# Dense chunk ahead of scores in every step of an attention stream, and maxima behind the dense part on VectorE

## The reference, cut to what matters

```
s = jnp.einsum('...qkgd,...skd->...kgqs', qg.astype(F32), kk.astype(F32)) * (ATTN_HEAD_DIM ** -0.5) + bias
s = jnp.where(valid, s, -jnp.inf)
sink = sinks.astype(F32).reshape(ATTN_KV_HEADS, ATTN_GROUP, 1)
m = jnp.maximum(jnp.max(s, axis=-1), sink)
e = jnp.exp(s - m[..., None])
p = e / (jnp.sum(e, axis=-1) + jnp.exp(sink - m))[..., None]
return jnp.einsum('...kgqs,...skd->...qkgd', p, vv.astype(F32))
...
x = x + o.astype(x.dtype) @ w_attn_out[j]
```

## Time and profile before

| | |
|---|---|
| median of three runs | 2412.86 us |
| lowest, highest run | 2411.56 us, 2414.92 us |
| the profiled execution | 2408.64 us |
| its span | 2406.8 us |
| TensorE busy | 2324.3 us (97%) |
| VectorE busy | 1489.9 us (62%) |
| ScalarE busy | 978.6 us (41%) |
| mean granted TensorE clock | 0.988 |

### The profile page before, as it was taken

One profiled execution on the slowest core, in us unless ns is written; L12 is line 12 of the kernel. 1 busy time (PEld: TensorE's weight loads), 2 busy tenths in 40 slices (PEclk: granted clock), 3 DMA queues, 4 the chain that ended last, 5 costly groups with the idle time before them and its releaser, 6 DMA issues.

```text
span 2406.8 us, 41163 instructions
## 1 busy us (share of the span) xinstructions
PE 2324.3 (97%) x16202; PEld 2219.4 (92%) x16202; DVE 1489.9 (62%) x2591; ACT 978.6 (41%) x1964; POOL 336.0 (14%) x334
## 2 busy tenths in 40 slices
PE   6999999998999999999998999999999999999998
PEld 6889898878999999999998977878999999999998
DVE  5545555569756656566566676465765656656564
ACT  4232222234535334343343354254633434435345
POOL 4000000013011111112112011013021111111113
PEclk7999999999999999999999999999999999999999
DMA  3112111101111121111111411101112112111121
GB/s 109 53 37 68 49 58 40 42 31 46 36 53 54 35 61 44 50 55 35 56 52 50 104 27 45 38 19 36 44 36 61 45 44 61 35 52 52 35 70 73
DMA packets 160983, 119.71 MB, mean 50 GB/s; under 512 B 23623, under 2 KB 140276, under 8 KB 160836
## 3 DMA queue, kind: packets, MB, share of 16 engines
q1 hardware_dynamic: 160724, 118.10, 16.7%
q10 hardware_dynamic: 144, 0.02, 0.0%
HBM read 110.94 MB, written 12.33 MB: 51 GB/s over the span
## 4 chain that ended last, share of the span: by engine, by line
PE 70%; issue 20%; DVE 5%; POOL 2%; ACT 1%; SPq 0%; POOLq 0%; DMA 0%; DVEq 0%; ACTq 0%
PE acc L2462 9%; PE acc L2464 9%; PE acc L2463 9%; PE acc L2422 8%; PE acc L2423 8%; PE acc L2424 8%; PE acc L2501 3%; PE acc L2503 3%; PE acc L2502 3%; PE acc L2520 2%; PE acc L2543 1%; PE acc L2400 1%; PE acc L2402 1%; PE acc L2401 1%; PE acc L2531 1%
## 5 line engine op out<-in xcount | busy, mean ns | idle before, releaser
L2462 PE MATMUL acc<-h_hi,w_hi 128*128 128x352 f32 x1440 | 464.6, 323 | 6.9 <-DVE x_res L1448 6.9
L2464 PE MATMUL acc<-h_hi,w_lo 128*128 128x352 f32 x1440 | 464.9, 323 | 0.0
L2463 PE MATMUL acc<-h_lo,w_hi 128*128 128x352 f32 x1440 | 462.8, 321 | 0.0
L1448 DVE TENSOR_TENSOR x_res<-x_res,acc 128x1056 f32<-128x1056 f32 x240 | 300.6, 1252 | 127.4 <-PE acc L2464 127.2
L2462 PEld LDWEIGHTS acc<-h_hi,w_hi 128*128 128x128 f32 x1440 | 270.2, 188 | 8.5 <-issue 6.6
L2464 PEld LDWEIGHTS acc<-h_hi,w_lo 128*128 128x128 f32 x1440 | 273.0, 190 | 0.0
L2463 PEld LDWEIGHTS acc<-h_lo,w_hi 128*128 128x128 f32 x1440 | 270.5, 188 | 0.0
L2422 PE MATMUL acc<-x_hi,w_hi 128*128 128x264 f32 x896 | 254.8, 284 | 0.0
L2424 PE MATMUL acc<-x_hi,w_lo 128*128 128x264 f32 x896 | 254.6, 284 | 0.0
L2423 PE MATMUL acc<-x_lo,w_hi 128*128 128x264 f32 x896 | 254.5, 284 | 0.0
L2179 PE MATMUL acc<-x_hi,w_hi 128*128 128x352 f32 x576 | 195.9, 340 | 4.2 <-DVE pair L1651 2.7
(11 more groups left out here) (334 smaller groups left out, 5237.5 us busy)
## 6 DMA issues: line engine op xcount, KB each, us to landing
w_raw<-in_w_up SPq DMA_DIRECT2D x64, 512.0 KB
w_raw<-in_w_down SPq DMA_DIRECT2D x64, 512.0 KB
w_raw<-in_w_mlstm_in SPq DMA_DIRECT2D x24, 512.0 KB
x_in<-in_x_prompt SPq DMA_DIRECT2D x8, 512.0 KB, 3.8
w_raw<-in_w_mlstm_out SPq DMA_DIRECT2D x8, 512.0 KB
w_raw<-in_w_q SPq DMA_DIRECT2D x16, 256.0 KB
w_raw<-in_w_attn_out SPq DMA_DIRECT2D x16, 256.0 KB
out_y_prompt<-y_out SPq DMA_DIRECT2D x8, 512.0 KB, 3.2
```

The costliest lines, as they stand in the source:

```text
L1448: V.tensor_tensor(blocks(x_res[:, k]), blocks(x_res[:, k]), row_banks(layer, k), ALU.add).then_inc(row_taken, 1)
L2462: T.matmul(out[:, b], hi[:, c], mh[:, span(b)], start=(c == 0), stop=False)
L2463: T.matmul(out[:, b], hi[:, c], ml[:, span(b)], start=False, stop=False)
L2464: x = T.matmul(out[:, b], lo[:, c], mh[:, span(b)], start=False, stop=(c == 1))
```

## The change

The two calls are exchanged on TensorE and on VectorE. On TensorE the dense chunks of a step come first, then the scores of unit u+1, the transposes, the values and the sample part. On VectorE the maxima of unit u+1 come behind the dense part instead of ahead of it. No instruction is added or removed, and ScalarE, GpSimd and the DMA queue keep their order.

```
@@ -2087,9 +2087,9 @@  (VectorE)
                     probabilities(u - 1)
                 if u >= 3:
                     outputs(u - 3)
+                att_dense(att_window(u))
                 if u + 1 < UNITS:
                     maxima(u + 1)
-                att_dense(att_window(u))
                 for gp in range(2):
                     sample(gp, u - SAMPLE_AT[gp])
```

## The result

| | before | after |
|---|---|---|
| median | 2413.89 us (6 runs) | 2421.88 us (6 runs) |
| lowest, highest | 2411.56, 2417.88 | 2420.04, 2425.84 |
| ratio | | 1.0034, 95% interval 1.0023 to 1.0045 |
| span of the profiled execution | 2406.8 us | 2418.1 us |

The change makes the kernel 8.0 us slower by the medians, 5.5 to 10.9 by the interval. The forecast was 10.6 us, 2423.5 as a time, added to the median of the three runs known then; with six runs the median before is 1.0 us higher.

A forecast was written before the change was run, and what follows sets the result against it. TensorE, busy 97% of the span, was taken as the bound, with gaps at array-shape changes. Terms 7.8 + 1.7 + 0.8 + 0.2 + 0.6 + 0.3 - 0.8 = 10.6 us, added to 2412.86, gave 2423.5 us; 80% range 2417.5 to 2428.5.

The forecast's parts named there:

- The extra change of shape: TensorE's steps with all four blocks: four array-shape changes instead of three, 0.17 us more in each of 46 steps, +7.8 us.
- The Trainium skill's price: Load of scores behind a dense chunk: by the skill's isolated-matmul latency 0.17 us later, not 0.11, making the shape term 2.8 us larger.
- Sample parts: Steps 24 to 29: TensorE's sample part waits for VectorE's, now behind the maxima; 3.2 us of waits against 1.5, +1.7 us.
- The chunk of step 32: This chunk waits for the low part of the first span's output, without scores ahead: 1.4 us against 0.6, +0.8 us.
- Step 36: Passage from full step 35 to an empty step: scores wait 1.4 us, transposes 0.3, 1.7 in place of 1.1, +0.6 us.
- Step 54: Passage from full step 53 to a step without chunk: scores and transposes wait 0.2 us each, 0.4 against 0.2, +0.2 us.
- Residual: Steps 39 and 42, VectorE's weight split ahead of the add TensorE awaits: +0.3 us in step 39, nothing in step 42.
- Start: Stream's start: step 0's chunk covers the scores' 0.88 us wait for maxima; first load to first transposes 5.0 against 5.82, -0.8 us.
- rival (C): TensorE's clock halves more often: two or three more falls of 3.4 us, each costing 1.7, 2427 to 2428.6 us; 14%.
- (A): TensorE's weight loads are pulled ahead, so the extra shape change costs nothing: +2.8 us, 2415.7 us; 6%.
- (B): VectorE's dense work becomes timely, removing every wait of steps with chunks: 5.2 us gain, 2407.7 us with shape change free; 4%.
- (D): Every added shape change on TensorE costs the widest gap: +15.2 us in place of 7.8, 2430.9 us; 4%.

## Why the prediction was right

*The extra change of shape* was the largest term, 7.8 us. The mechanism is shown, by a run that adds only it (6.5 us) and by a matmul of 64 rows against one of 128. Its size was a little over: 0.17 us a step, 0.15 measured (3.18 us in 21 steps), so 46 x 0.15 = 6.9 us. Chunk to scores, 1.65 us in the stream's first step, is 1.63 in the plain step, and the two starts behind it came 0.01 closer each. Of the bounds, 0.11 and 0.33, the measured value lies near the lower.

*The Trainium skill's price.* In the changed kernel the loads of the scores show the gap of 0.22 us behind the chunk again in every step, that of the earlier trace rows, and the term came out under the rows' sum, not over it. The 2.8 us more that the prediction worked out from the Trainium skill's TensorE: Matmul & The Clock Gate, Single matmul latency, are not there.

*Sample parts.* Forecast 3.2 us of waits in steps 24 to 29 in place of 1.5. Measured 0.53, 0.84, 0.55, 0.56 and 0.79, 3.3 us in all, and 0.27 in step 30, which had been hidden before behind half clock. Right, term by term.

*The chunk of step 32.* Forecast +0.8, measured 1.25 against 0.61, +0.6.

*Step 36.* Forecast a wait of 1.7 in place of 1.1, through GpSimd's old read of `q_t`. Measured:

```profile
1501.37 1.39 DVE L1963 SCALAR_TENSOR_TENSOR q_t<-acc,rstd 128x352 f32<-128x352 f32 x3 [2.67 <-POOL o_lo L1334]
...
1504.14 0.70 PE L2520 MATMUL acc<-k_t,q_t 64*128 64x256 f32 x4 [1.60 <-DVE stat L1997]
```

The moves wait for GpSimd, the scores wait 1.60 us for the maxima behind them, and the transposes' load another 0.1 (a gap of 0.43, where the plain one is 0.33). +0.5.

*Step 54.* Forecast +0.2, from two waits of 0.2 in place of one. Measured +0.1. The view of TensorE's waits shows neither wait, for the modelled ends of the matmuls ahead hide them. The loads show both, 0.2 and 0.1 us beyond the plain gaps of 0.17 and 0.33:

```profile
1609.43 0.30 PEld L2520 LDWEIGHTS acc<-k_t,q_t 64*128 64x128 f32 x4 [0.38 <-DVE stat L1997]
...
1610.16 0.42 PEld L2531 LDWEIGHTS acc<-ident,prob 128*128 128x128 f32 x4 [0.43 <-DVE prob L2007]
```

*Residual.* This step failed: +0.3 was forecast, and the two waits are 0.30 and 0.53 us, where they were 0.33 and 0.57. I had strung the durations of probabilities and outputs together, 0.88 and 0.28 us. In step 39 of the changed kernel their starts lie closer than their ends: the reciprocal starts at 1525.73, the outputs at 1526.46 and the split at 1526.66, 0.93 us and not 1.16. Start-to-start times should have been taken, as for TensorE.

*Start.* Forecast -0.8, measured -0.86.

*Sum.* Measured terms: -0.9 + 6.9 + 1.8 + 0.3 + 0.6 + 0.5 + 0.1 = 9.3 us, inside the interval of 5.5 to 10.9. All terms but the sample parts' came out under their forecast, so the sum isn't right by errors that cancel. The 0.3 in it is the wait of step 30, which the prediction didn't have.

*The clock* makes up the rest of the profiled difference of 11.3 us. Before, it fell in step 30; after, not there but behind the wait of 1.4 us in step 64:

```profile
1637.00:1640.00 3.00, 2.98 (x12) 0.55 0.00 0
```

That is -1.7 and +1.5 us, and one more fall behind the stream, at 1706 us, some 1.7. The 11.3 us are more than the 8.0 of the medians since the profiled execution before lies 5.2 us under its median and the one after 1.8. In rival (C) more waits were to bring more falls; in the changed kernel there were two where there had been one, and the half-clock stretches of the runs above vary as much. One execution of each can't say whether the change does that.

*The signs named ahead.* The four gaps, the sample parts' waits in both spans, the waits of steps 36 and 54 and the start came as forecast; the plain step is 3.44 us and not 3.47, the chunk of step 32 waits 1.25 and not 1.4. One sign of a wrong forecast came too: the time outside the stream moved, by 2.0 us. The fall at 1706 us accounts for most of it, and it is the clock's, which the sum left out.

*Rivals.* (A), loads pulled ahead across a change of shape, is out: at every change of the plain step the load starts together with its first matmul, 2 to 3 ns apart by the medians, where from the chunk to the transposes, without a change, it starts 0.16 us ahead of it. (B), a gain by timely dense work, named waits that did shrink (start, step 36's transposes), but they came back at the scores and the sample parts. (D), the widest gap for each change, is out by the measured 0.15.

## What to carry to other kernels

Read TensorE's list as a sequence of array shapes, not only of dependencies: here 64-row, 64-column and full matmuls in turn paid some 0.15 us for each change added, in gaps that no wait and no busy time shows, so put neighbours of one shape together and count the changes in a loop's cycle. A block whose result is wanted a step later may go anywhere by its dependencies, and still cost by where it stands. A short wait can hide behind the modelled end of a matmul, so ask for the waits of the weight loads too. Before an order on one engine is changed, look also for what it will run beside on GpSimd: here a scaling that started just behind a long GpSimd instruction lasted as long as that one.

## What the hardware showed that was not expected

- VectorE's `TENSOR_SCALAR` on 128x256 float32 took 0.35 us by its median and up to 2.42 us beside GpSimd's subtraction of 2.36; one wait more on GpSimd took 6.7 us off TensorE's waits. In the kernel before the same blocking is there, in five scalings of 1.3 to 1.42 us, but nobody waits; in the changed kernel no scaling takes over 0.66.
- All eleven falls to half clock inside the stream, in the twelve traces, came right behind a wait of 1.0 to 2.4 us among small matmuls; nine were 3.4 us long, one 10.2 and one 13.7. Not each such wait has one: the 1.60 us of step 36 in the changed kernel had none behind it, and 1.62 us at the same place in the run with the sample part ahead of the maxima had. In the kernel before, steps 55 to 63 had eight waits of 0.3 to 0.8 us, and the clock stayed at 1.00.
- The gap at a change of shape went by what ran ahead of it, whatever shape followed: 0.17 us behind 128-column transposes and values, 0.22 behind the 352 columns of a chunk, 0.33 behind the 256 columns of the scores, and 0.04 behind the small matmul of 64 rows and 32 columns.
